# Hybrid attention encoder on one core: the scores of an attention step moved behind its values and turns

## The reference

```python
x = x + 0.5 * swiglu(rmsnorm(x, g_ff1[l]), w1_ff1[l], w3_ff1[l], w2_ff1[l])
h = rmsnorm(x, g_mix[l])
p = h @ w_in[l]                       # q, k, v of three branches, and three gates
o_a = diff_attention(...)             # 4 heads, softmax of two maps, a - lam * b
o_b = neighborhood_attention(...)     # 8 heads on a 64-wide grid
o_c = dilated_attention(...)          # 8 heads, three windows combined
g = jax.nn.sigmoid(gates.reshape(B, S, N_BRANCH, D))
merged = (g[:, :, 0] * (o_a @ w_br_a[l]) + g[:, :, 1] * (o_b @ w_br_b[l])
          + g[:, :, 2] * (o_c @ w_br_c[l]))
x = x + merged @ w_o[l]
x = x + 0.5 * swiglu(rmsnorm(x, g_ff2[l]), w1_ff2[l], w3_ff2[l], w2_ff2[l])
```

## Time and profile before

| what | value |
|---|---|
| median of three runs | 1283.6 us |
| profiled execution, own time | 1283.66 us |
| its span | 1281.6 us |
| TensorE busy (PE) | 1268.4 us, 99% |
| weight loads (PEld) | 1081.8 us, 84% |
| VectorE busy (DVE) | 868.9 us, 68% |
| ScalarE busy (ACT) | 682.0 us, 53% |
| GpSimd busy (POOL) | 42.1 us, 3% |
| granted TensorE clock, mean | 0.998 |

### The profile page before, as it was taken

One profiled execution on the slowest core, in us unless ns is written; L12 is line 12 of the kernel. 1 busy time (PEld: TensorE's weight loads), 2 busy tenths in 40 slices (PEclk: granted clock), 3 DMA queues, 4 the chain that ended last, 5 costly groups with the idle time before them and its releaser, 6 DMA issues.

```text
span 1281.6 us, 17701 instructions
## 1 busy us (share of the span) xinstructions
PE 1268.4 (99%) x6822; PEld 1081.8 (84%) x6822; DVE 868.9 (68%) x1238; ACT 682.0 (53%) x925; POOL 42.1 (3%) x57
## 2 busy tenths in 40 slices
PE   8999999999999999999999999999999999999997
PEld 5888888888888888888888888888888888888886
DVE  5666667556987775666676665765578887655665
ACT  6454555445866454445554445554477653644444
POOL 0411100000000000000000000000000000000000
PEclk9999999999999999999999999999999999999999
DMA  8787855564645545555455555465555355455550
GB/s 282 230 260 245 262 213 197 191 216 147 235 121 175 176 182 192 181 188 186 177 194 197 196 182 182 160 217 192 183 200 203 124 177 185 181 197 196 196 192 37
DMA packets 59212, 245.07 MB, mean 191 GB/s; under 512 B 21344, under 2 KB 27616, under 8 KB 32408
## 3 DMA queue, kind: packets, MB, share of 16 engines
q1 hardware_dynamic: 58144, 242.54, 54.5%
q10 hardware_dynamic: 984, 1.80, 0.4%
q0 software_dynamic: 32, 0.02, 0.0%
HBM read 239.07 MB, written 5.27 MB: 191 GB/s over the span
## 4 chain that ended last, share of the span: by engine, by line
PE 98%; DVE 1%; DMA 0%; issue 0%; ACT 0%; POOLq 0%; POOL 0%; SPq 0%; DVEq 0%; ACTq 0%
PE bank L769 30%; PE bank L703 17%; PE bank L705 16%; PE bank L704 16%; PE bank L773 15%; PE bank L1066 1%; PE bank L827 1%; PE bank L1080 1%; PE bank L835 0%; DMA params<-in_params 0%; DVE x L1518 0%; PE bank L723 0%; PE bank L731 0%; PE bank L915 0%; PE bank L907 0%
## 5 line engine op out<-in xcount | busy, mean ns | idle before, releaser
L1178 DVE TENSOR_TENSOR wlo<-raw,whi 128x2048 fp32r<-128x2048 f32 x209 | 479.3, 2295 | 274.2 <-ACT whi L449 269.5
L449 ACT ACTIVATE whi<-raw 128x2048 fp32r<-128x2048 f32 x206 | 393.3, 1912 | 228.0 <-PE bank L773 141.9
L769 PE MATMUL bank<-xT,whi 128*128 128x512 f32 x1664 | 414.8, 391 | 0.0
L769 PEld LDWEIGHTS bank<-xT,whi 128*128 128x128 f32 x1664 | 301.8, 188 | 55.7 <-issue 0.9
L773 PEld LDWEIGHTS bank<-xT,wlo 128*128 128x128 f32 x1664 | 220.2, 190 | 12.8
L773 PE MATMUL bank<-xT,wlo 128*128 128x256 f32 x1664 | 224.1, 282 | 0.0
L703 PE MATMUL bank<-whi,xT 128*128 128x512 f32 x432 | 171.7, 397 | 0.0
L705 PE MATMUL bank<-whi,xT 128*128 128x512 f32 x432 | 168.5, 390 | 0.0
L704 PE MATMUL bank<-wlo,xT 128*128 128x512 f32 x432 | 168.3, 390 | 0.0
L703 PE MATMUL bank<-whi,hTh 128*128 128x512 f32 x320 | 124.6, 390 | 0.0
L704 PE MATMUL bank<-wlo,hTh 128*128 128x512 f32 x320 | 124.5, 389 | 0.0
(11 more groups left out here) (171 smaller groups left out, 1145.2 us busy)
## 6 DMA issues: line engine op xcount, KB each, us to landing
raw<-in_stream SPq DMA_DIRECT2D x209, 1024.0 KB, 4.8
bias<-t_rows SPq DMA_DIRECT2D x24, 256.0 KB, 6.5
bias<-in_rpb SPq DMA_DIRECT2D x16, 256.0 KB, 7.8
masked<-bias SPq DMA_DIRECT2D x8, 512.0 KB, 6.9
bias<-masked SPq DMA_DIRECT2D x8, 512.0 KB, 4.6
raw<-in_stream SPq DMA_DIRECT2D x10, 256.0 KB, 6.2
x<-in_x SPq DMA_DIRECT2D x4, 256.0 KB, 5.2
raw<-in_stream ACTq DMA_DIRECT2D x2, 256.0 KB, 4.3
```

The lines of the kernel that those rows point to most:

```text
L449: act.activation(whi[:, s, :], raw[:, s, :], ACT.Copy).then_inc(hi_ready, 1)
L769: return pe.matmul(dst[blk][:, :], whi[:, s, w], xT[:, 4 * a + k, :, :].rearrange("p a s -> p (a s)"), start=start, stop=stop)
L1178: dve.tensor_tensor(wlo[:, s, :], raw[:, s, :], whi[:, s, :].bitcast(F32), ALU.subtract).then_inc(unit_split, 1)
```

## The change

TensorE's program alone changes, in its loop over the steps: behind the dense unit come now the values of pair j-2, then the turns of pair j-1, and the scores of pair j last. The waits inside these three functions are as they were.

```diff
                         unit_rows(l, U_MIX + j, 0, th, tl, k0, pr, True, True, before=before, mid=turn_first)
-                    if j < PAIRS:
-                        scores(j)
                     if 2 <= j < PAIRS + 2:
                         values(j - 2)
                     if 1 <= j <= PAIRS:
                         turn_probs(j - 1)
+                    if j < PAIRS:
+                        scores(j)
                     if j == PAIRS + 2:
                         turn_o(0)
                         turn_o(1)
```

## The result

The changed kernel takes 1306.32 us (median of four runs, 1305.42 to 1307.7) against 1283.77 us of the kernel before on the same chip: a ratio of 1.0169, 95% interval 1.0157 to 1.0181. It is slower by 22.5 us; 1300.1 was forecast, with a range of 1291 to 1306, at whose upper edge the time lies.

The account below looks back on a forecast made before the run. TensorE, busy without a gap, bounds the kernel; the new order makes turns wait for the 8.04 us chain. Pairs 1-7 5.67, pair 8 1.77, pair 10 0.83, pair 11 0.14, less 0.18: 8.23 a layer, 1283.66 to 1300.1 us, range 1291 to 1306.

Parts of the forecast that it names:

- The ring: Attention stage: scores now stand behind waiting turns, so each wait delays the next release; period 9.69 against 8.88 us, +0.81.
- The chain: ScalarE and VectorE work from release (`pair_to_hi` start, behind scores) to the normalising's end, which turns need: 8.04 us, unchanged.
- 6.53 - 6.30 = 0.23: Pair 11: probabilities usable 6.53 us after release, turns reached at 6.30; less 0.09 for seams, +0.14 us.
- the sum: Attention stage's step-by-step additions over pairs 0 to 11: 8.23 us a layer, 16.5 for two.
- Rivals 1 and 2: Turns: no waits, only seams saved, 1281.5 us, 6%; or VectorE's 0.75 us wait for `pTh` goes, 1288.1 us, 6%.
- rival 3: TensorE's clock falls to 1.2 GHz in part of the stage; in a quarter of 22 steps 25 us, about 1325; 3%.
- the sign "stays at 1.00": Predicted sign in the profile after: TensorE's clock should stay at 1.00.
- the sum's own terms (5.55 + 0.89 + 0.36 + 0.09 + 0.91): TensorE step in us: dense unit 5.55, branch A's values 0.89, four turns 0.36, seam into scores 0.09, scores 0.91.
- The seams saved, 0.09 a step: TensorE's extra time where matmul kind changes; the new order was to save 0.09 us a step, alone at pairs 0 and 9.
- rival 4: Dearer wait: hand-back to TensorE and seam into scores at upper bounds, 0.3 us more in ten steps a layer; 1306; 8%.
- What was cost at nothing: Earlier values, weights' low parts, `add_bias`, `pair_to_lo` and SyncE's loads in the attention stage: expected covered, adding no time.

Follow-up runs that it names:

- The half change: Changed kernel with values first but scores ahead of the turns again: 1286.14 us against 1284.84 of the kernel before, ratio 1.0011.
- the shorter chain: Changed kernel with VectorE taking the weights' low part behind the normalising or mixing in steps 0 to 11: 1297.58 us, ratio 1.0108 to the kernel before.
- the longer chain: Two more VectorE subtracts (1.2 us) in steps 1 to 8, added to the kernel before (1288.54 us) and to the changed kernel (1325.36 us).

## Why the prediction was right, and what it mis-sized

**What bounds it, and the mechanism: right.** The ring scores, chain, turns, scores sets the period of pairs 1 to 8. The chain kept its 8.04 us, `pTh` its 2.34; the waits stand at the turns of pairs 1 to 8, 10 and 11, none at 0 and 9; that of pair 11, 0.26 us, is close to the 6.53 - 6.30 = 0.23 of the sum. The half change takes the waits away, the shorter chain takes them away where nothing else is disturbed, and the longer chain is paid one for one in the new order and hardly in the old. Rivals 1 and 2 fall with this: nothing of VectorE's 0.75 us for `pTh` went.

**The size: 8.23 us a layer were forecast, 10.85 came.** The terms that differ:

- *The clock, rival 3, held at a quarter of the stage or not at all; the sum and the sign "stays at 1.00" had it at nothing.* It fell once in each layer, behind the wait of 1.65 to 1.69 us. The interval from pair 9's release to pair 10's is 9.49 us, where the sum's own terms (5.55 + 0.89 + 0.36 + 0.09 + 0.91) give 7.80; with the wait filled it takes 8.29, so 1.20 of it is the clock. Three runs agree on this net price: 1.23 us a layer from the filled wait, 1.15 between the two layers of the run with the low part late in step 8, 1.26 between those of the longer chain. This is a little under half of the missing 2.6 us. I had taken the opening, 8.17 us busy of 10 at a clock of 1.00, as evidence against any fall; its longest gap was 1.53. By the sum, pairs 1 to 8 would hide a slow unit inside the chain; no trace has a fall there. The Trainium skill, TensorE: Matmul & The Clock Gate, "A second HAM failure mode: psum-queue depth-cycling", was the rule that spoke for it; the run with the gap filled agrees in kind (1.23 us a layer back), though not in extent, since seven shorter waits a layer brought no fall.
- *The seams saved, 0.09 a step: wrong.* Without a wait a step of the new order takes 8.92 us, measured where the low part comes late, against 8.79 by my terms and 8.88 of the old order. The period with a wait is 9.74 to 9.80 against 9.69, which makes 0.5 us a layer in pairs 1 to 7. The seam from turns into scores, which no row showed, holds 0.08 of the 0.13 a step: in that run the turns take 0.97 to the next scores (355.18 to 356.15), 0.17 more than to a unit, where I took 0.09.
- *Pair 9's step, 7.80 by the terms, is 8.29 at full clock.* I had the wait of pair 8's values for VectorE's `split_o` at nothing; with the seams it makes another 0.5 us a layer.

So of the 21.7 us that the two stages lost, 16.5 are the ring as worked out, some 2.5 the clock, and the 2.7 that are left I put down to the seams and to pair 9's step, of which the runs show some 2. The forecast's range ended at 1306.0, the figure of rival 4, the same sum with 0.3 us of dearer seams a step. The runs show 0.05 to 0.13 a step, so that the time comes out at that edge is in part luck.

**What was cost at nothing: right here, but thin.** Weights, bias loads and `add_branch` came in time in the changed kernel, and of `split_o`'s wait nothing was felt there, since the slow unit covers it. Three of the experiments moved one VectorE instruction of 2.29 us past `add_branch` or past a slot's release, and each time a unit or a bias was late by 1.2 to 7.4 us.

## What to carry to other kernels

An engine that is busy without a gap can still be one instruction's move from being bound by a ring over other engines: before moving a producer closer to its consumer in program order, write down the chain from its release to its consumer and the work that covers it, and remember that a wait in a ring comes back in every turn. When a wait must be cured by moving work on another engine, list what that engine does next and which queue waits for it; three cures here moved the wait elsewhere. And price a gap of TensorE with the unit behind it as well, at the lower clock.

## What the runs showed of the hardware

- In the changed kernel an idle time of 1.69 us in the first layer and of 1.65 in the second was followed by TensorE's lower level, 1.2 GHz (matmuls of 512 columns every 0.43 us, some eight and some five of them, and in the second layer scores before them); with the gap filled by 14 matmuls the clock stayed at 1.00 in both. The opening's gap of 1.53 us in the kernel before left it at 1.00 too. But the length of a gap alone doesn't tell. In the run with the longer chain a wait of 2.33 us left the clock at 1.00 and one of 2.32 at the same place in the second layer brought it to 0.50 (the turns' rows, and busy time by stretch):

```profile
398.51 0.63 PE L1066 MATMUL bank<-ident,probs 128*128 128x128 f32 x4 [2.33 <-DVE probs L1495]
...
1049.14 1.09 PE L1066 MATMUL bank<-ident,probs 128*128 128x128 f32 x4 [2.32 <-DVE probs L1495]
```
```profile
398.00:400.00 2.00, 1.49 (x17) 1.22 (x17) 1.56 (x3) 0.00 (x0) 0.00 (x0) 1.00 0.81 344
1049.00:1051.00 2.00, 1.86 (x12) 1.56 (x14) 1.19 (x2) 0.00 (x0) 0.00 (x0) 0.50 0.95 397
```

Waits of 0.71 and 1.26 us close together, in the run with the low part late in step 8, did the same: down in one layer and not in the other. What else decides was not tried.
- A fall behind pair 8 cost 1.15 to 1.26 us a layer net, less than the 1.56 by which its unit was slower.
- From the turns into the 64-row scores a step takes 0.17 us more than from the turns into a unit.
